# Attention over a prompt: the softmax sums' guard in one branch of four, and reciprocals moved ahead of a copy

## What is computed

```python
def masked_softmax(logits, mask):
    l = jnp.where(mask, logits.astype(jnp.float32), -jnp.inf)
    m = jnp.max(l, axis=-1, keepdims=True)
    m = jnp.where(jnp.isfinite(m), m, 0.0)
    e = jnp.where(mask, jnp.exp(l - m), 0.0)
    return e / jnp.maximum(jnp.sum(e, axis=-1, keepdims=True), 1e-30)
...
    pc = masked_softmax(lc, dc >= 0)
...
    ps = masked_softmax(ls.reshape(B, NSA_KV_HEADS, NSA_GROUP, Tq, n_k), ms)
...
    pw = masked_softmax(lw, (dw >= 0) & (dw < WINDOW) & (wpos[None, :] >= 0))
...
    p = masked_softmax(l, kpos[None, :] <= qpos[:, None])
```

## Time and profile before

| what | value |
|---|---|
| time, median of 3 runs (lowest, highest) | 2436.97 us (2434.25, 2440.63) |
| the profiled execution's own time | 2431.19 us |
| its span in the profile | 2429.4 us |
| busy over the span: PE, weight loads, DVE, ACT, POOL | 96%, 62%, 51%, 23%, 34% |
| the stage, 340 to 742 us: PE, DVE, ACT, POOL busy | 329.2, 276.3, 250.3, 191.8 us |

### The profile page before, as it was taken

One profiled execution on the slowest core, in us unless ns is written; L12 is line 12 of the kernel. 1 busy time (PEld: TensorE's weight loads), 2 busy tenths in 40 slices (PEclk: granted clock), 3 DMA queues, 4 the chain that ended last, 5 costly groups with the idle time before them and its releaser, 6 DMA issues.

```text
span 2429.4 us, 32589 instructions
## 1 busy us (share of the span) xinstructions
PE 2323.7 (96%) x11863; PEld 1511.0 (62%) x11863; DVE 1235.8 (51%) x3115; ACT 552.4 (23%) x1328; POOL 835.1 (34%) x874
## 2 busy tenths in 40 slices
PE   8999997888888999899999999999999999999999
PEld 4544665545546677688886458888888874443343
DVE  4876726776773444522322794433334324229765
ACT  0001016666663333111111221111011110001131
POOL 0000004544454000475753454334333227203531
PEclk9999999999999999999999999999999999999999
DMA  5423720021028877632325301111111115544201
GB/s 185 106 82 86 273 104 29 2 91 49 2 64 222 232 232 198 204 91 78 87 71 158 83 31 53 36 36 53 35 44 44 36 49 200 176 143 139 80 18 57
DMA packets 185961, 240.38 MB, mean 99 GB/s; under 512 B 53435, under 2 KB 128833, under 8 KB 184265
## 3 DMA queue, kind: packets, MB, share of 16 engines
q1 hardware_dynamic: 181018, 218.99, 29.5%
q0 software_dynamic: 3616, 9.73, 1.2%
q10 hardware_dynamic: 1168, 9.58, 1.1%
HBM read 216.18 MB, written 37.99 MB: 105 GB/s over the span
## 4 chain that ended last, share of the span: by engine, by line
PE 56%; DVE 2%; ACT 1%; issue 0%; DVEq 0%; ACTq 0%
PE ps L2225 36%; PE ps L2389 11%; PE ps L2278 5%; PE ps L2446 2%; PE ps L2376 1%; DVE xT L153 1%; PE ps L2454 1%; ACT xT L2499 0%; PE ps L2282 0%; DVE arena L2977 0%; ACT arena L2596 0%; DVE stats L2651 0%; PE ps L2321 0%; DVE xT L1380 0%; DVE queries L2980 0%
## 5 line engine op out<-in xcount | busy, mean ns | idle before, releaser
L2225 PE MATMUL ps<-xT,arena 128*128 128x272 f32 x1920 | 472.7, 393 | 1.7 <-DVE arena L1382 1.7
L2225 PEld LDWEIGHTS ps<-xT,arena 128*128 128x128 f32 x1920 | 363.9, 190 | 77.3 <-DVE arena L1382 2.1
L2225 PE MATMUL ps<-queries,arena 128*128 128x272 f32 x1312 | 332.5, 393 | 1.9 <-PEq L1422 1.0
L2225 PEld LDWEIGHTS ps<-queries,arena 128*128 128x128 f32 x1312 | 249.6, 190 | 54.0 <-DVE queries L2792 1.4
L236 PE MATMUL ps<-arena,xT 128*128 128x512 f32 (+1 forms) x512 | 198.9, 552 | 0.8 <-issue 0.8
L1015 POOL TENSOR_SCALAR arena<-arena,gates 128x55 f32<-128x55 f32 (+15 forms) x192 | 123.4, 652 | 172.1 <-DVE arena L914 172.1
L950 ACT ACTIVATE arena<-arena 128x640 f32<-128x640 f32 (+15 forms) x256 | 164.2, 642 | 72.3 <-DVE arena L906 41.5
L236 PEld LDWEIGHTS ps<-arena,xT 128*128 128x128 f32 x512 | 98.3, 192 | 101.1 <-issue 94.3
L786 PE MATMUL ps<-arena,queries 64*128 64x512 f32 (+11 forms) x704 | 128.8, 467 | 24.7 <-DVE arena L906 15.7
L2225 PE MATMUL ps<-arena 128*128 128x272 f32 x576 | 148.4, 394 | 0.0
L2389 PE MATMUL ps<-arena 128*128 128x512 f32 x312 | 140.6, 599 | 0.0
(11 more groups left out here) (345 smaller groups left out, 3286.8 us busy)
## 6 DMA issues: line engine op xcount, KB each, us to landing
arena<-in_cache_fox_kv SPq DMA_DIRECT2D x72, 256.0 KB, 4.4
arena<-in_w_ffn_down SPq DMA_DIRECT2D x68, 256.0 KB, 3.3
arena<-in_w_in SPq DMA_DIRECT2D x16, 1024.0 KB, 5.2
xT<-in_w_ffn_down SPq DMA_DIRECT2D x64, 256.0 KB, 3.5
xT<-in_cache_fox_kv SPq DMA_DIRECT2D x56, 256.0 KB, 6.5
arena<-in_cache_nsa_kv SPq DMA_DIRECT2D x64, 192.0 KB, 8.6
arena<-in_w_ffn_up SPq DMA_DIRECT2D x11, 1024.0 KB, 5.5
arena<-in_w_ffn_gate SPq DMA_DIRECT2D x11, 1024.0 KB
```

Source lines behind the costliest of these rows:

```text
L2225: mm = pe.matmul(ps[:, first + BANK_OF[z], 0:PIECE], weight[:, j, :], moving[:, j, :], start=(j == 0 and z in (1, 6, 5, 7)), stop=(j == kk ...
```

## The change

`invert` keeps the guard, and the wait behind it, for the pairs of the compressed branch alone; a new table `GUARDS` counts the guards up to each pair, as not every pair raises the count now. In the loop of DVE `invert` of pair p+2 comes ahead of the copy of p's second chunk; for pairs with one chunk the order stays as it was.

```diff
+GUARDS = [sum(q.branch == CMP for q in PAIRS[:n]) for n in range(NPAIR + 1)]
...
             def invert(p):
                 dve.wait_ge(exp_done, 2 * p.n + 2)
                 s = sums[:, p.n % 4, :]
-                nc.vector.tensor_scalar(s, s, TINY, None, ALU.max).then_inc(guarded, 1)
-                dve.wait_ge(guarded, p.n + 1)
+                if p.branch == CMP:
+                    nc.vector.tensor_scalar(s, s, TINY, None, ALU.max).then_inc(guarded, 1)
+                    dve.wait_ge(guarded, GUARDS[p.n + 1])
                 nc.vector.reciprocal(s, s).then_inc(inverse_ready, 1)
...
                 save(p, 0)
                 if p.n + AHEAD < NPAIR:
                     logits(PAIRS[p.n + AHEAD])
+                if p.n + AHEAD - 1 < NPAIR:
+                    invert(PAIRS[p.n + AHEAD - 1])
                 if len(p.chunks) > 1:
                     save(p, 1)
-                if p.n + AHEAD - 1 < NPAIR:
-                    invert(PAIRS[p.n + AHEAD - 1])
```

## The result

The changed kernel takes 2415.25 us, the median of five runs (2412.85 to 2419.16). The kernel before takes 2434.25 us (five runs, 2428.9 to 2440.63; the three of the prediction are among them). The recorded ratio is 0.9927, with a 95% interval of 0.9913 to 0.9942: faster by 0.73%. It is an estimate of its own and not the quotient of the two medians. The direction is as forecast. The time is not: 2415.25 lies 12.75 us under the 2428.0 of the forecast and 4.75 us under the low end of its range.

A forecast was written before the change was run, and what follows sets the result against it. Bound: in prompt attention PE waits for POOL, which waits for DVE's guard and reciprocal. Removed chain guards give 7.0 + 2.6 = 9.6 us at most, 8.3 at least; taking 9.0, 2436.97 - 9.0 = 2428.0 us, range 2420 to 2436.

The forecast's parts named there:

- The chain and its guards: Prompt attention's repeating loop of scores, logits, guard, reciprocal, multiplies, transposes; 43 removed guards on it give 8.3 to 9.6 us.
- Held by POOL: Eight removed chain guards that ended with POOL's instruction; each removal saves 0.32 us of idle POOL, 2.6 us together.
- Plain: 35 removed chain guards not held by POOL, or nearly so; each removal brings the reciprocal 0.20 us earlier, 7.0 us together.
- tight joint: In the 256-key tile two removals (0.40 us) meet only 0.25 us of PE idle, twice, taking off 0.3 us.
- The reorder: Reciprocal ahead of DVE's second-chunk copy in 48 pairs of over 512 keys; copy 0.40 us later, gain counted as 0.
- a lost cover: If the 3.5 us between copy and PE's transposes were gone, 48 copies at 0.2 to 0.45 us cost up to 16.
- Behind the stage: After prompt attention the gain passes on; the first late load's 2.27 us PE wait grows 0.4 us at worst.
- The list of what would show it: Signs of being right, such as 32 guards left and PE's POOL wait down some 8 us, and signs of being wrong.
- The second chain: Other inputs within 0.1 us at half the stage's joints leave about 4.5 us of gain, time 2432.5; chance 0.25.
- "It does nothing": The trace names the wrong releaser for the chain, or loads behind lose the gain; time 2437; chance 0.06.
- the slower rival: The 32 remaining compressed-branch guards become held by POOL, 0.8 us more each, 26 us together; time 2454; chance 0.06.
- rival 2: Less PE waiting removes five half-clock pieces of the stage, giving 4.7 us more, time about 2423; chance 0.15.

The follow-up runs named there:

- the two guards: The kernel before with a second guard behind the first in all pairs but the compressed ones: median 2444.78 us, 2439.4 at clock 0.990.
- the stand-in: The changed kernel with a second reciprocal into a spare place, and its wait, where each removed guard was: median 2431.89 us, 2429.3 at clock 0.990.
- The 57 runs: Runs of the kernel before, nothing changed, recorded with the follow-up experiments on three chips: median 2431.93 us, 2430.9 at clock 0.990.
- the diagonal early: The changed kernel with POOL's diagonal sum moved from a tile's first WIN pair to its first SLC pair, except the first tile: median 2416.06 us, 2417.9 at clock 0.990.

## Why the prediction was wrong

**What held.**
- *The chain and its guards.* Walked back in the timeline, it passed 43 removed guards; their sum was put at 9.0 us, between 8.3 and 9.6. At equal clock the runs show 9.9 +- 0.4, without the reorder 9.7; that is 0.3 above the 9.6 that the prediction called the most that can be had, within the error. The doubled guards gave 8.5, where 43 x 0.20 is 8.6. The four tiles at full clock gave 2.48 of 2.76.
- *What lies off the chain.* 28 more guards gone gave 0.9 +- 0.6, not 5.6.
- *The two kinds of guard.* Their split came out otherwise, their sum did not; that the two misses cancel is luck. Held by POOL: 8 x 0.32 = 2.6 forecast, 1.6 +- 0.5 measured. Plain: 7.0 forecast, 8.3 measured. The tiles at full clock agree on the held ones: the four have 12 of the chain's removed guards, three of them held, and 2.48 us are 0.21 for each, the held ones no dearer than the plain. What lacks is where the held ones are (512 keys: 1.03 of 1.24; 256 keys: 0.79 of 0.92, where the prediction had also seen a tight joint).
- *The reorder.* Counted at 0, measured 0.3 +- 0.4; the copies come later, and PE's wait for DVE's copies stayed (6.3 us, 6.2 before). The price that the prediction put on a lost cover is mis-multiplied (48 x 0.45 us are 21.6, not 16); nothing hangs on it, as the cover held.
- *Behind the stage.* The first wait for a load didn't grow: it was 2.27 us and is 1.71 in the changed kernel's timeline. A second one, of 1.12 us at 782.35, is new; together they are 0.6 us more, where the prediction had 0.4 at the worst. The gain still passes on: from the last turn to the end the changed kernel is 2.1 us shorter, not longer.
- *The list of what would show it.* 32 guards, 5.3 us; POOL's idle time between the diagonal's sum and the multiply behind it gone (0.33 us before); PE's wait for POOL down by 8.1. One of its signs of being wrong came too, the other number of stretches at 0.50.

**Rivals.** The second chain (4.5 us) falls: 9.9 us came through, so PE's other inputs took next to nothing of it. "It does nothing" falls. The guards that stay are not held (166 ns at most), so the slower rival falls too. The rule of the Trainium skill behind it ("SBUF — State Buffer", section "Who interferes with whom") is borne out where a guard does meet POOL: 1.12 us at most with all guards kept. It didn't decide here, as none of the 32 was lengthened.

**The step that failed** is the one ahead of the sum: "at unchanged clock". The forecast took the granted clock as given, and made its rise a rival of 0.15, at 4.7 us. The runs show a rise in the mean of the kernels with a shorter chain: seven such sets (41 runs, 0.9905 to 0.9932 by set) have a mean clock of 0.9916 +- 0.0003, before 0.9895 +- 0.0003, and the two guards 0.9863 +- 0.0008. Filling PE's idle time alone, with the chain no shorter than before, raised it to 0.9933 +- 0.0006; taking the guards away but not PE's wait (the stand-in) left it at 0.9888 +- 0.0007. So the clock goes with PE's waiting, not with the guards as such. The size that the rival had worked out from the earlier trace rows, 4.7 us, was about right: 0.0021 x 1.66 per 0.001 are 3.5 us, from the eleven runs of the changed kernel 4.0. In part that is luck: its five pieces were a guess, and its 0.94 us for one of 3.4 us is low beside 1.37 in the tile above and 1.2 by the line (3.41 x 0.34).

**The second error** is the base. The median of three runs was 2436.97, and the prediction noted that the profiled run was 5.8 us below it without asking what set the two apart. The 57 runs have a median of 2431.93, and only two of them lie at 2436.97 or above. On the line 2436.97 would be a clock of 0.986; but the clocks of those three runs are not on record, so why they lay high stays open.

The miss of 12.75 us is thus made of: base 5.0 (2436.97 less 2431.93); clock 6.1 ((0.9932 - 0.9895) x 1.66 per 0.001), of which about 2 were the luck of these five runs and some 4 come with the change; chain 0.9 (9.9 less 9.0). Together 12.0; 0.7 is left over. With the corrected base, and the forecast's own 9.0 and 4.7 added, the prediction would have been 2418.2, beside 2417.65 in eleven runs.

**The range** had the clock's rise in it: its low end, 2420, is rival 2 less the scatter. It failed by the base from which that was counted. From 2431.93 the same low end is 2415.0, and the 2415.25 would have lain just inside; the eleven runs' 2417.65 lies 2.4 us under the 2420 as it stood.

What stays open: which stretches fall to half clock. The two behind the stage went too, in work that the edit doesn't touch. The one ahead of the stage, at about 239 us, is in seven of the fourteen profiles (3.4 or 6.8 us) and not in the other seven, while the program ahead of the stage is the same in all. And the mean clock of one kernel differs from run to run by up to 0.009. Only means over many runs were compared.

## What to carry over

In a stage like this one, where PE waits often at its joints, a change that shortens the waiting can raise the granted clock as well: work out the sum at unchanged clock, then add what the half-clock stretches cost, as the likeliest case and not as an aside. Compare kernels at equal clock, by the line of time over mean clock from many runs of one of them; a median of three runs carries its draw of the clock. And cost a small instruction with a wait behind it by its step along the chain (here 0.20 us, 43 of 96), not by its number.

## What was not expected of the hardware

The mean granted clock follows PE's waiting even where nothing of PE's own work changes: 43.0 us of waiting for POOL in the stage went with 0.9863, 33.0 with 0.9895, 24.9 with 0.9919 (eleven runs); with the idle time filled, 16.2 went with 0.9933. The waits are of one profile each, the clocks means of all runs. It isn't the wait for POOL alone (17.8 us with the diagonal early went with 0.9912), and one set of five or six runs can be 0.001 off. And a reciprocal of 128x2 numbers on DVE isn't held by POOL where the `tensor_scalar` of the same size is: 0.167 us at most in 128, beside 1.12.
